# Two 64-block solve steps and the a by k products of the other array half, in turns; copies and masks reordered

## The reference

```python
def step(S, inp):
    r_t, w_t, k_t, v_t, a_t, b_t = inp
    sa = jnp.einsum("bhij,bhj->bhi", S, a_t)
    S = S * w_t[:, :, None, :] + sa[..., None] * b_t[:, :, None, :] + v_t[..., None] * k_t[:, :, None, :]
    return S, jnp.einsum("bhij,bhj->bhi", S, r_t)
```

## Time and profile before

| | |
|---|---|
| median of 3 runs | 735.41 us |
| profiled execution | 734.78 us, span 733.0 us |
| TensorE busy | 723.5 us (99%) |
| VectorE busy | 561.0 us (77%) |
| ScalarE busy | 434.1 us (59%) |
| GpSimd busy | 48.4 us (7%) |
| granted clock of TensorE | 0.998 of full speed |

### The profile page before, as it was taken

One profiled execution on the slowest core, in us unless ns is written; L12 is line 12 of the kernel. 1 busy time (PEld: TensorE's weight loads), 2 busy tenths in 40 slices (PEclk: granted clock), 3 DMA queues, 4 the chain that ended last, 5 costly groups with the idle time before them and its releaser, 6 DMA issues.

```text
span 733.0 us, 16878 instructions
## 1 busy us (share of the span) xinstructions
PE 723.5 (99%) x7266; PEld 590.6 (81%) x7266; DVE 561.0 (77%) x895; ACT 434.1 (59%) x688; POOL 48.4 (7%) x83
## 2 busy tenths in 40 slices
PE   9999999999999999999999999999999999999997
PEld 6888878888688888888878685898888888865553
DVE  6689978877789999997668788899684676763453
ACT  5689974425748666766647562486573755653342
POOL 0000124040020000000002000003003000000000
PEclk9999999999999999999999999999999999999999
DMA  9990306230776755565871732348335354466001
GB/s 345 377 394 21 112 18 237 113 114 6 255 228 206 231 183 177 217 230 173 298 277 54 290 131 102 117 151 310 116 132 213 114 216 173 190 230 244 15 1 58
DMA packets 64170, 129.52 MB, mean 177 GB/s; under 512 B 1888, under 2 KB 24928, under 8 KB 63712
## 3 DMA queue, kind: packets, MB, share of 16 engines
q1 hardware_dynamic: 63056, 126.06, 48.1%
q0 software_dynamic: 320, 1.67, 0.7%
q10 hardware_dynamic: 720, 0.71, 0.3%
HBM read 127.39 MB, written 1.05 MB: 175 GB/s over the span
## 4 chain that ended last, share of the span: by engine, by line
PE 85%; DVE 8%; DMA 3%; ACT 3%; issue 1%; SPq 0%; DVEq 0%
PE bank L628 38%; PE bank L750 14%; PE bank L3218 11%; PE bank L2538 3%; PE bank L1564 3%; DMA ring<-in_w_in_dram 3%; PE bank L1545 2%; PE bank L885 2%; DVE arena L574 1%; PE bank L1822 1%; DVE arena L1127 1%; PE bank L1889 1%; PE bank L1988 1%; DVE arena L616 1%; PE bank L1876 1%
## 5 line engine op out<-in xcount | busy, mean ns | idle before, releaser
L628 PE MATMUL bank<-hg,arena 128*128 128x256 f16 x2496 | 275.0, 273 | 0.2 <-DVE hg L653 0.2
L628 PEld LDWEIGHTS bank<-hg,arena 128*128 128x128 f16 x2496 | 243.9, 98 | 30.6 <-issue 1.1
L574 DVE SCALAR_TENSOR_TENSOR arena<-ring,arena 128x1024 f16<-128x1024 f32 x150 | 175.6, 1226 | 58.8 <-ACT arena L542 58.8
L542 ACT ACTIVATE arena<-ring 128x1024 f16<-128x1024 f32 x150 | 146.7, 1044 | 86.4 <-PE bank L3218 37.6
L3218 PE MATMUL bank<-arena 128*128 128x512 f16 (+1 forms) x480 | 83.6, 336 | 0.0
L3218 PEld LDWEIGHTS bank<-arena 128*128 128x128 f16 x480 | 47.0, 98 | 36.1
L750 PE MATMUL bank<-arena 128*128 128x256 f16 x528 | 57.8, 273 | 0.0
L750 PEld LDWEIGHTS bank<-arena 128*128 128x128 f16 x528 | 51.7, 98 | 6.0
L561 DVE SCALAR_TENSOR_TENSOR arena<-ring,arena 128x2048 f16<-128x2048 f32 x22 | 50.4, 2292 | 0.7
L750 PE MATMUL bank<-mix,arena 128*128 128x256 f16 x384 | 42.2, 273 | 0.0
L554 ACT ACTIVATE arena<-ring 128x2048 f16<-128x2048 f32 x22 | 41.7, 1894 | 0.0
(11 more groups left out here) (415 smaller groups left out, 961.7 us busy)
## 6 DMA issues: line engine op xcount, KB each, us to landing
ring<-in_w_in_dram SPq DMA_DIRECT2D x12, 2048.0 KB, 10.7
ring<-in_ffn_w_up_dram SPq DMA_DIRECT2D x22, 1024.0 KB, 7.7
ring<-in_w_ff_dram SPq DMA_DIRECT2D x8, 2048.0 KB, 9.3
ring<-in_w_ff_dram SPq DMA_DIRECT2D x16, 1024.0 KB, 6.6
ring<-in_ffn_w_down_dram SPq DMA_DIRECT2D x11, 1024.0 KB, 6.2
ring<-in_w_out_dram SPq DMA_DIRECT2D x8, 1024.0 KB, 7.6
ring<-in_w_xk_dram SPq DMA_DIRECT2D x2, 2048.0 KB, 12.3
ring<-in_w_xv_dram SPq DMA_DIRECT2D x2, 2048.0 KB, 10.9
```

The costliest lines, as they stand in the source:

```text
L542: nc.scalar.activation(quarter(halves_of(chunk)[0], chunk, q), quarter(slot(*chunk), chunk, q), ACT.Copy, scale=W_SCALE).then_inc(*mark("w ...
L574: nc.vector.scalar_tensor_tensor(quarter(halves_of(chunk)[1], chunk, q), quarter(slot(*chunk), chunk, q), W_SCALE, quarter(halves_of(chunk ...
L628: mm = nc.tensor.matmul(out_, weight[a][:, k, cols], src[:, k, b, :], start=(first and i == 0), stop=(last and i == 2), skip_group_check=True)
```

## The change

TensorE: each of the two 64-block steps now has the AK products of one half among it. After every second P64 matmul one AK product of half 1 follows (`key_product(1, ...)`), after every second dXT64 matmul one AK product of half 0. The separate run of AK products is gone. `fill(12)` moves from behind RK to between the two steps, G is done for half 1 first, and P64 waits at its start for X64 of half 1 too. VectorE: the P64 and XT64 copies leave it; in chunk 0 `dve_ssd_end` comes right behind the X64 copies; the AK masks go half 1 first; pieces of `wout_low` and `dve_ssd_low` move behind the RB masks, one piece to the start of chunk 1, and `wout_low(1, (0, 1))` behind the y copy. (`mem_low(dve, 8)` did nothing before: there are 8 quarters, 0 to 7.) ScalarE: it gets the P64 and XT64 copies, and in chunk 0 the two `wout_high` pieces go behind the G and U copies. The number of products, masks and split pieces is the same.

```diff
@@ -1920,17 +1920,28 @@
+            def key_product(g, j):
+                lo = 64 * g
+                mm = nc.tensor.matmul(quarters(3 * g + 1)[:, j, :], KT_[lo:lo + 64, j, c * C:(c + 1) * C],
+                                      AT_[lo:lo + 64, j, c * C:(c + 1) * C], start=True, stop=True)
+                if j == 3:
+                    mm.then_inc(*mark("solve_pe", "AK bank", c, g))
             for g in range(2):
...
                 pe.wait_ge(*at("X64 diagonal", c, g))
+                if g == 0:
+                    pe.wait_ge(*at("X64", c, 1))
                 for j in range(4):
...
                                           st["X64"][0:64, j, :], start=True, stop=True)
-                mm.then_inc(*mark("solve_pe", "P64 bank", c, g))
-            products(c, 1, KT_, AT_, "AK bank")
-            fill(11)
+                    if j == 3:
+                        mm.then_inc(*mark("solve_pe", "P64 bank", c, g))
+                    if j % 2:
+                        key_product(1, 2 * g + j // 2)
+            fill(12)
             for g in range(2):
@@ -1939,13 +1950,15 @@
                                           st["XT128"][64:128, j, 64:128], start=True, stop=True)
-                mm.then_inc(*mark("solve_pe", "dXT64 bank", c, g))
+                    if j == 3:
+                        mm.then_inc(*mark("solve_pe", "dXT64 bank", c, g))
+                    if j % 2:
+                        key_product(0, 2 * g + j // 2)
...
             products(c, 0, KT_, RT_, "RK bank")
-            fill(12)
-            for g in range(2):
+            for g in (1, 0):
                 pe.wait_ge(*at("AK", c, g))
@@ -2047,6 +2060,7 @@
                 dve_mem_keys(dve, 1)
+                wout_low(dve, 0, (1,))
             for n, m in enumerate(LEVELS):
@@ -2096,44 +2110,28 @@
                     "p (j n) -> p j n", j=4)).then_inc(*mark("solve_vector", "X64", c, g))
-            for g in range(2):
-                dve.wait_ge(*at("P64 bank", c, g))
-                nc.vector.tensor_copy(P64[g][64:128, :, :],
-                                      banks[3 * g][64:128, 0:256].rearrange("p (j m) -> p j m", j=4)).then_inc(
-                    *mark("solve_vector", "P64", c, g))
-            if c:
-                mem_low(dve, 8)
-            else:
+            if c == 0:
                 dve_ssd_end(dve)
-            for g in range(2):
+            for g in (1, 0):
                 dve.wait_ge(*at("AK bank", c, g))
...
             for g in range(2):
-                dve.wait_ge(*at("dXT64 bank", c, g))
-                nc.vector.tensor_copy(sets[g]["XT128"][0:64, :, 64:128],
-                                      banks[3 * g + 2][0:64, 0:256].rearrange("p (j m) -> p j m", j=4)).then_inc(
-                    *mark("solve_vector", "XT64", c, g))
-            for g in range(2):
                 dve.wait_ge(*at("RK bank", c, g))
...
                     *mark("solve_vector", "RK", c, g))
-            if c:
-                wout_low(dve, 0, (2, 3))
-                dve_ssd_low(dve)
-            else:
-                wout_low(dve, 0, (0,))
             for g in range(2):
...
             if c:
+                dve_ssd_low(dve)
+                wout_low(dve, 0, (2, 3))
                 dve_mem_keys(dve, 3)
-                wout_low(dve, 1, (0, 1))
             if c == 0:
-                wout_low(dve, 0, (1,))
                 mem_low(dve, 4)
+                wout_low(dve, 0, (0,))
                 for g in range(2):
@@ -2144,6 +2142,8 @@
                 *mark("solve_vector", "y out", c, 1))
+            if c:
+                wout_low(dve, 1, (0, 1))
@@ -2168,7 +2168,6 @@
                 mem_high(act, 4)
-                wout_high(act, 0, (0, 1))
             else:
@@ -2178,10 +2177,20 @@
             for g in range(2):
+                act.wait_ge(*at("P64 bank", c, g))
+                nc.scalar.activation(P64[g][64:128, :, :], banks[3 * g][64:128, 0:256].rearrange(
+                    "p (j m) -> p j m", j=4), ACT.Copy).then_inc(*mark("solve_act", "P64", c, g))
+            for g in range(2):
+                act.wait_ge(*at("dXT64 bank", c, g))
+                nc.scalar.activation(sets[g]["XT128"][0:64, :, 64:128], banks[3 * g + 2][0:64, 0:256].rearrange(
+                    "p (j m) -> p j m", j=4), ACT.Copy).then_inc(*mark("solve_act", "XT64", c, g))
+            for g in range(2):
                 st = sets[g]
...
                                      ACT.Copy).then_inc(*mark("solve_act", "G", c, g))
+            if c == 0:
+                wout_high(act, 0, (0,))
             for g in range(2):
@@ -2189,6 +2198,8 @@
                 wout_high(act, 1, (0, 1))
+            else:
+                wout_high(act, 0, (1,))
             act.wait_ge(*at("y bank", c, 0))
```

## The result

The kernel before took 735.1 us (734.66 to 736.79). The changed one took 761.99, 753.13, 762.57 and 743.22 us, median 757.56: 3.1% above the median of before. The forecast was 743.3, its range 738.5 to 747.5. The median lies outside. The ratio is 1.018 [1.014, 1.022]; the two runs near 762 don't count in it, since such comparisons set aside runs far above the fastest of the same kernel, though here the change itself makes them slow. The four times go with the mean granted clock of each run: 0.972, 0.985, 0.972 and 0.999. At 0.999 the kernel takes 743.22 us.

What follows compares the result with a forecast made beforehand. TensorE, busy 723.5 of 733.0 us, was taken as the bound; turns 6.3, X64 wait 0.7 and y stall 0.9 (+7.9) took the profiled 734.8 to 742.7, plus 0.6 for the median: 743.3 us, range 738.5 to 747.5.

Steps and rivals of the forecast that it cites:

- The shapes: TensorE in both chunks' sections: tile shape changes at every turn, a section 3.18 us, +3.13 a chunk, +6.3 us for two.
- The price of a change in a short turn: In both sections: each shape change costs 0.14 into 64x64, 0.20 into 64x128; bounds -0.7 to +0.4 us a chunk.
- the y stall: Chunk 1, VectorE's w_out pieces behind the y copy: the y-back transposes wait, +0.9 us, bounds 0 to 1.2.
- X64's wait: Start of section one: TensorE waits for the X64 copy of half 1, +0.37 us, +0.7 for two chunks.
- The copies, masks and orders at 0: Copies moved to ScalarE, AK mask order and VectorE's reordering apart from the y copy's delay: covered, taken as 0.
- The sum: Whole kernel: 6.3+0.7+0.9 = +7.9 us, giving a median of 743.3 us.
- 1: Rival, turns of both sections: halves don't wait for each other, whatever the shapes; 734.9 us, no change; chance 0.10.
- 2: Rival, sections: passes mix across shapes, one more round trip for each of 16 key pieces, 5.4 us: 748.7; chance 0.05.
- 3: Rival: turns cost as forecast but VectorE's and ScalarE's work hides both waits, 741.7 us; 0.15 of the forecast's 0.8.
- 4: Rival: VectorE or ScalarE becomes late as well (masks, copies), 1 to 3 us more, 745 to 746; chance 0.05.

Runs made afterwards that it cites:

- e1: Changed kernel with each key (AK) product as two 64x64 tiles in place of one 64x128: 735.75 us, ratio 1.0007 to the kernel before.
- e10: Changed kernel with the X64 wait behind the first two P64 and `wout_low(1, (0, 1))` back ahead of the y copy: 749.07 us, ratio 1.017.
- e4: VectorE's and ScalarE's order of the changed kernel with TensorE's order of the kernel before: 736.14 us, ratio 1.0012.
- e3: TensorE's order of the changed kernel with the old VectorE and ScalarE functions of the kernel before: 754.15 us, ratio 1.023.
- e5: The changed kernel run again as it is, against the kernel before: 752.95 us, ratio 1.019.
- e7: Changed kernel with turns in section one (P64) only, section two's key products in one group behind dXT64: 742.86 us, ratio 1.0098.
- e2: Changed kernel without turns, the four key products of a half in one group behind its solve step: 739.47 us, ratio 1.0058.

## Why the prediction was wrong

**The shapes.** Right, and to 0.01: turns of 0.37 and 0.42, a section 3.19, RK 0.89, G 1.93. The price of a change in a short turn, which I took from longer pieces, is the same in the short ones. The Trainium skill (TensorEngine Tiling (Array Packing), Tiling Modes, Key Properties) says that going to another tiling mode drains the engine. The trace agrees, also where the two kinds sit on different halves of the array: 3.19 us a section, against 1.1 in e1.

**The waits and the y stall.** X64's wait is 0.43 for a forecast of 0.37, the y stall 0.91 for 0.9; e10 took both away and came to 741.56 at full clock, 1.7 under 743.2.

**The copies, masks and orders at 0.** Right: e4, all of them together, costs 0.8 to 0.9 with the y stall in it.

**The sum.** 743.3 forecast; the three runs at a clock of 0.997 or more took 743.22, 743.61 and 744.55.

**The step that failed** is one the working doesn't have. It opens with "at a granted clock of 1.00 (the 2.4 GHz level)" and then sums all of the new order with durations read at that level. The order it sums for halves TensorE's work per microsecond in the sections (24 records in 3.18 us, for 32 in 2.16 before), and I never asked if the clock would stay. It fell in seven of ten runs and cost 9 to 19 us: more than the whole forecast loss. The Trainium skill (TensorE: Matmul & The Clock Gate, What's actually happening) says that the clock goes by how busy the engine has been of late. The busy share of the profile would not have foretold it here: in e10 the clock falls at 122.7 with TensorE busy in all of the 5.00 us around it (120 to 125). A rival with a fall in each chunk, as the runs now show it, would have been 743 + 19 = 762, and the runs hold it twice. It could not be priced from the trace of the kernel before, which stays at 1.00 in both stages; but it was put at nothing without a reason.

**The rivals.** 1 (halves overlap whatever the shapes) was wrong, and e1 is what it describes once the shapes agree. 2, 3 and 4 did not come.

## What to carry to other kernels

In this kernel, matmuls on separate parts of the array overlapped only when their tiles had the same shape. Before you take two kinds in turns, cut them to one shape, and count every change that is left at 0.11 to 0.25 us. When an edit puts many changes of shape close together, put a term for the clock into the sum, time it in several runs and read the granted clock of each, since the busy share doesn't show it. A gain of a microsecond on TensorE is kept only if the other engines' queues are moved with it: here it came back first as a late y copy and then as a late weight transfer.

## What the runs showed of the hardware

- The granted clock halved for 17 or 24 us at a stretch with TensorE busy 24.00 of 24.00 us, elsewhere for 3.4 us (e3, e5, e7, e10). The place differs from run to run (both chunks in the change's profile, at 123.1 and 177.6; of the sections of e5 those of chunk 1 alone), and 4 pieces a section in place of 8 kept it in all five runs.
- Tiles of one shape but different column counts (64x64 and 64x128 outputs, both from 64x64 weights) overlap: 32 records on two halves in 1.1 us, 16 in 1.11 alone (e2).
- At the half clock not everything doubles: a turn goes from 0.79 to 1.34 us, 16 records of G from 1.93 to 3.60, the 48 of y from 2.92 to 3.89 with the clock back at the end.
